# Wide products for ten projection tiles of a block attention, and a longer warming run, in a two-model fp32 kernel

## The chip, the cores and the metric

The kernel runs on one core of one Trainium2 chip as one launch. The metric is the device time of that core in microseconds (us), lower is better; a kernel's time is the median of several executions. One execution was also recorded by the hardware profiler, and all rows below are of that one. Times inside it count from the start of its span.

## The reference

Two transformer-like blocks are applied to one sequence of 256 tokens of width 1024, all in fp32. The first has two gated feed-forward layers around a mixer (Fourier mixing and grouped attention). The second has two layers, and the change is in the attention of its second one:

```python
def shared_kv(x, kv_norm, w_kv, cos, sin):
    k, v = jnp.split(rms_norm_2(x, kv_norm) @ w_kv, 2, axis=-1)
    k = apply_partial_rope(k.reshape(bsz, seq, N_HEADS, HEAD_DIM_2), cos, sin)
    ...
def moba_attention(h, w_q, w_o, cos, sin, k_blk, v_blk, k_mean):
    q = apply_partial_rope((h @ w_q).reshape(bsz, seq, N_HEADS, HEAD_DIM_2), cos, sin)
    ...
x = x + moba_attention(h, moba_w_q[j], moba_w_o[j], cos, sin, k_blk, v_blk, k_mean)
x = x + mem_cross_attention(rms_norm_2(x, norm_mem[l]), rms_norm_2(mem, norm_memkv[l]),
                            mem_w_q[l], mem_w_kv[l], mem_w_o[l])
```

There are 8 heads of 128 and blocks of 256 tokens. The sequence is one block, so each query sees its own block alone, under a causal mask. The keys of the memory attention that follows (`m` below) depend on the memory alone and are projected during the block attention.

## The kernel before

**Tiles and their split.** All weights are laid out by the host as 205 tiles of 128 x 16 x 128 fp32 numbers (1 MB each), in the order in which they are used (`STREAM`). Tile `t` lies in slot `t % 3` of three buffers. For each one SyncE loads `raw`; ScalarE writes the rounded high half to `wt[:, 0]` (`split` of ScalarE, line 972, semaphore `weight_hi`); VectorE writes the remainder `raw - high` to `wt[:, 1]` (`split` of VectorE, line 1340, semaphore `weight_lo`). An operand (`xn`, `mn`, `h`) is held in the same way as a high part and a rest. A product in fp32 accuracy is then high x high + high x rest + remainder x high.

**Wide and narrow.** A tile gives two blocks of 128 outputs (`m`) for 256 tokens and has 8 steps of the inner dimension (`k`). *Wide*, the high weights multiply high part and rest of the operand side by side in one product of 512 columns (line 424), and the remainder multiplies the high part in one of 256 columns (line 482) that lands on the columns of the rest: 16 + 16 products per tile. The bank holds two halves, which have to be added when it is emptied. *Narrow*, all three products have 256 columns and land on the same columns (lines 469 and 482): 48 products per tile, and one instruction empties the bank. In both forms `square_tile` waits for `weight_hi` before its first product and for `weight_lo` before its first product with the remainder. For value tiles the operand is the stationary side and the weights move. Their narrow form (`narrow_values`, lines 504 and 509) waits for `weight_hi` first and for `weight_lo` after its 32 products with the high half. Their wide form (the rest of `value_tile`, lines 527 and 530) moves high half and remainder side by side and waits for `weight_lo` before its first product.

**Emptying.** In the block attention (`moba`) the k and m tiles are emptied by VectorE (`scaled`, line 1469: times the norm factor), and the q and v tiles by ScalarE alone (lines 997 and 1002, semaphore `copied_out`). Wide tiles elsewhere: ScalarE copies the rest half to one of three `rest` buffers (`rest`, lines 984 and 988), VectorE adds it (`whole_of`, line 1460; for values line 1580), and the semaphore `drained` counts them.

**Order in the block attention stage.** Each engine has one program order, written out by hand. The tiles are `MOBA`: k0, k1, v0, q0, q1, k2, q2, v1, k3, q3, v2, v3, m0, m1. TensorE does the first five, then the scores of heads 0 and 1, and from there on the other tiles in pieces (`PIECES`) between the steps of the 8 heads: transposing the probabilities (line 835), the scores of two heads later (line 819), the product with the values (line 847). VectorE gives each q and k tile a rotation (`turn`, lines 1601 to 1604), and for each head takes the maxima, normalises the probabilities (line 1674) and makes the rest of the output (`rest`). Between these stand its splits: `after(t)` is the split of tile t + 2. So the split of tile 5 (k2) stands behind the turn of q0, that of tile 7 (v1) behind the turn of k2, and those of tiles 9 to 13 one each behind the maxima of a head. For a head's scores TensorE waits until its q tile is turned, and for its value product until the v tile is drained.

**Start.** While the first loads are under way, TensorE multiplies `ones` by `ones` `WARM` times (line 856). One such fp32 product shows as two records.

Of the kernel before, what the change touches and what calls it, by code (L numbers as in the profile page):

```python
# [10 lines left out]
ACT = mybir.ActivationFunctionType  # L11
AX = mybir.AxisListType

P = 128
S = 256
# [3 lines left out]
NT = S // P  # L19
TILE = 16  # L20
RING = 3
FF = 22
WARM = 10
KEEP = 7
LAST = 2752 % P
UPPER, LOWER = slice(0, LAST), slice(LAST, P)
# [6 lines left out]
MOBA = [("k", 0), ("k", 1), ("v", 0), ("q", 0), ("q", 1), ("k", 2), ("q", 2), ("v", 1), ("k", 3), ("q", 3), ("v", 2), ("v", 3),  # L33
        ("m", 0), ("m", 1)]
# [13 lines left out]
FIRST, COUNT = {}, {}  # L48
# [26 lines left out]
]  # L75


NARROW = ("w_in", "moba")
PAIR, OUT, EMPTIED, REST, RESTS, TAKEN = {}, {}, {}, {}, [], {}
_taken = 0  # L80
_count, _emptied = {"drained": 0, "copied_out": 0}, {}
for _name, _pairs in PAIRS:
    for _j, _p in enumerate(_pairs):
        PAIR[_name, _j] = _p
        EMPTIED[_name, _j] = _emptied.get(_p)
        if _name in ADD:
            _emptied[_p] = ("added", KP * ADD[_name] + _j + 1)
            continue
        _by = "copied_out" if _name == "moba" and MOBA[_j][0] in "qv" else "drained"
        _count[_by] += 1  # L90
        OUT[_name, _j] = _emptied[_p] = (_by, _count[_by])
        if _name.startswith("gu"):
            _taken += 1
            TAKEN[_name, _j] = _taken
            _emptied[_p] = ("taken", _taken)
        if _name not in NARROW:
            REST[_name, _j] = len(RESTS)
            RESTS.append((_name, _j))

# [53 lines left out]
SPREAD_AT = {n: i + 1 for i, n in enumerate(SPREADS)}  # L153
# [21 lines left out]
def program(nc, weights, x_t, mem_t, vectors, consts, fourier, fnet_w, positions, out_t):  # L175
    ctx = ExitStack()
    with ctx:
# [14 lines left out]
        q_t = sb("q_t", [P, KB, S])  # L192
        k_t = sb("k_t", [P, KB, S])
        v_s = sb("v_s", [P, NT, D])
# [17 lines left out]
        col_x = sb("col_x", [P, NT])  # L212
# [32 lines left out]
        def pair_banks(name, j):  # L245
            return bank[:, 2 * PAIR[name, j]:2 * PAIR[name, j] + 2, :]
# [17 lines left out]
        def pair(b):  # L264
            return slice(2 * b, 2 * b + 2)
# [11 lines left out]
        tile_done = sem("tile_done")  # L277
        taken, rest_copied, drained, copied_out = sem("taken"), sem("rest_copied"), sem("drained"), sem("copied_out")
# [6 lines left out]
        factor, spread, spread_taken = sem("factor"), sem("spread"), sem("spread_taken")  # L285
# [135 lines left out]
        def _(pe):  # L421
# [91 lines left out]
            def value_tile(t, out, a, beside={}, ks=(0, KB), narrow=False):  # L513

                w = wt[t % RING][:].rearrange("p a (m k) c -> p a m k c", m=2)
                if narrow:
                    narrow_values(t, out, a, w, beside, ks)
                    return
                o = [out[:, n, :].rearrange("p (a m c) -> p a m c", a=2, m=2) for n in range(NT)]
                tok = [slice(n * P, (n + 1) * P) for n in range(NT)]  # L520
                if ks[0] == 0:
                    pe.wait_ge(weight_lo, t + 1)
                for k in range(*ks):
                    if k in beside:
                        beside[k]()
                    for n in range(NT):
                        pe.matmul(o[n], a[:, k, 0, tok[n]], w[:, :, :, k, :], start=k == 0, stop=False, skip_group_check=True)  # L527
                for k in range(*ks):
                    for n in range(NT):
                        mm = pe.matmul(o[n][:, 1], a[:, k, 1, tok[n]], w[:, 0, :, k, :], start=False, stop=k == KB - 1,  # L530
                                       skip_group_check=True)
                if ks[1] == KB:
                    mm.then_inc(tile_done, 1)
# [208 lines left out]
            def part(kind, j, ks=(0, KB), **more):  # L742
                what = PARTS[kind][j][0]
                t, out = FIRST[kind] + j, banks_for(kind, j, ks[0] == 0)
                if kind == "moba":
                    src = h[:, KB:2 * KB] if what == "q" else mn if what == "m" else xn
                else:
                    src = xn if what == "q" else mn
                if what == "v":
                    value_tile(t, out, src, ks=ks, beside=more.get("beside", {}), narrow=kind in NARROW)  # L750
                else:
                    square_tile(t, out, src, ks=ks, narrow=kind in NARROW, **more)

            def pieces(kind, n, i, ready):
                for j, k0, k1 in PIECES[kind][n][i]:
# [141 lines left out]
            for j in range(5):  # L897
                square_tile(FIRST["w_in"] + j, banks_for("w_in", j), xn, ready=operand("mix") if j == 0 else None, narrow=True,
                            late=None if j else KP * OPERAND["mix"],
                            beside={**norm("mix").get(j, {}), **sums_beside.get(j, {}), **({4: head_factors} if j == 4 else {})})  # L900
# [6 lines left out]
            for g in range(4):  # L907
                f_s, out = probs[g % 2], seq[g % 2]
# [19 lines left out]
            for j in range(COUNT["conv_in"]):  # L928
                square_tile(FIRST["conv_in"] + j, banks_for("conv_in", j), xn, ready=operand("mix0") if j == 0 else None,
                            cuts=() if j else (4, 6), late=None if j else KP * OPERAND["mix0"],  # L930
                            beside={1: {5: both_sums}, 2: {1: lambda: spread_factor("mix0")}, 3: {1: lambda: spread_column(col_1, SPREAD_AT["mix0 first"], 0)}}.get(j, {}))
# [16 lines left out]
            for j in range(AHEAD["moba"]):  # L948
                part("moba", j, **({0: dict(ready=operand("kv"), late=KP * OPERAND["kv"]), 3: dict(ready=operand("mix1"))}.get(j, {})),
                     beside=norm("mix1").get(j, {}))  # L950
# [10 lines left out]
        def _(act):  # L961
# [15 lines left out]
            def rest(name, j, col=None, factors=0):  # L977

                i, src = REST[name, j], pair_banks(name, j)[:, :, S:2 * S]
                act.wait_ge(tile_done, FIRST[name] + j + 1)  # L980
                if i >= 3:
                    out_of(act, *RESTS[i - 3])
                if col is None:
                    act.activation(rest_s[i % 3][:], src, ACT.Copy).then_inc(rest_copied, 1)  # L984
                else:
                    act.wait_ge(factor, factors)
                    for n in range(NT):
                        e = act.activation(rest_s[i % 3][:, n, :], src[:, n, :], ACT.Copy, scale=col[:, n:n + 1])
                    e.then_inc(rest_copied, 1)

            def rest_part(kind, j):
                what, i = PARTS[kind][j]
                if kind == "moba":
                    src = pair_banks(kind, j)
                    if what == "q":
                        act.wait_ge(tile_done, FIRST[kind] + j + 1)
                        act.activation(q_t[:, pair(i), :], src[:, :, 0:S], ACT.Copy).then_inc(copied_out, 1)
                    elif what == "v":
                        act.wait_ge(tile_done, FIRST[kind] + j + 1)
                        act.wait_ge(factor, SPREAD_AT["mix1"])  # L1000
                        for n in range(NT):
                            e = act.activation(v_s[:, n, 2 * P * i:2 * P * (i + 1)], src[:, n, 0:S], ACT.Copy, scale=col_x[:, n:n + 1])
                        e.then_inc(copied_out, 1)
                elif what != "v":
                    rest(kind, j)
                else:
                    rest(kind, j, col_m, SPREAD_AT["mem"])

# [210 lines left out]
            for j in range(3):  # L1219
                after(FIRST["w_in"] + j)  # L1220
                out_of(act, "w_in", j)
                src = gk_t if j == 0 else q_t[:, 2 * j - 2:2 * j, :]
# [46 lines left out]
            for p in range(KP):  # L1269
                for m in range(2):  # L1270
                    k, j = 2 * p + m, 3 * p + m
# [56 lines left out]
        def _(dve):  # L1328
# [135 lines left out]
                    e.then_inc(told, 1)  # L1464

            def scaled(name, j, dst, r):
                if name in NARROW:
                    dve.wait_ge(tile_done, FIRST[name] + j + 1)
                    dve.tensor_tensor(dst, pair_banks(name, j)[:, :, 0:S], both(r), ALU.mult).then_inc(drained, 1)
                    return  # L1470
                whole_of(name, j, dst)
                dve.tensor_tensor(dst, dst, both(r), ALU.mult).then_inc(drained, 1)
# [97 lines left out]

            def part(kind, j):
                what, i = PARTS[kind][j]
                if OUT[kind, j][0] == "copied_out":
                    return
                of_memory = what == "m" if kind == "moba" else what != "q"
                if what == "v":
                    col, src, at = col_m if of_memory else col_x, pair_banks(kind, j), REST[kind, j]
                    dve.wait_ge(rest_copied, at + 1)
                    for n in range(NT):
                        e = dve.scalar_tensor_tensor(v_s[:, n, 2 * P * i:2 * P * (i + 1)], src[:, n, 0:S], col[:, n:n + 1],  # L1580
                                                     rest_s[at % 3][:, n, :], ALU.mult, ALU.add)
                    e.then_inc(drained, 1)
                elif what == "q":

                    whole_of(kind, j, q_t[:, pair(i), :], drained)
                else:
                    scaled(kind, j, k_t[:, pair(i), :], (r_m if of_memory else r_x)[:])
# [272 lines left out]
            for p in range(KP):  # L1860
                for m in range(2):
                    k, j = 2 * p + m, 3 * p + m
# [18 lines left out]
                j = 3 * p + 2  # L1881
# [66 lines left out]
            m, y, t = (root[:, i, 0:NT] for i in range(3))  # L1948
# [131 lines left out]
```

## Time and profile before

| | before |
|---|---|
| median of 3 executions | 1235.22 us (1235.21 to 1235.88) |
| profiled execution, its own time | 1236.79 us |
| its span, first to last instruction | 1235.0 us |
| TensorE busy (products) | 1227.8 us, 99% |
| VectorE busy | 929.0 us, 75% |
| ScalarE busy | 660.0 us, 53% |
| read from memory | 219.52 MB, 179 GB/s over the span |

The span lies 1.8 us under the profiled execution's own time. Busy shares are means over stages with different limits; the page's slices and the timelines show them stage by stage. The end of a product is modelled, so that neighbouring products overlap in the records: what tells their pace is the distance from start to start.

### The profile page before, as it was taken

What the parts mean: (1) busy time and instruction counts of PE and PEld (TensorE: products, weight loads), DVE (VectorE), ACT (ScalarE), POOL (GpSimd) and SP (SyncE); (2) the same over time, 40 slices, a digit from 0 to 9 for tenths busy, and PEclk for the clock granted to TensorE, in tenths of its full rate; (3) what the DMA queues carried; (4) which work ended last, traced back from release to release, by engine and by line L of the source; (5) the groups of instructions that cost most, each with busy time, mean ns of one, the idle gap of its engine ahead of it and who ended that gap; (6) DMA issues with size and microseconds to landing.
All of it is one profiled execution on the core that took longest, in us unless ns stands there. A gap on an engine that the chain in (4) does not pass through costs nothing.

```text
span 1235.0 us, 18032 instructions
## 1 busy us (share of the span) xinstructions
PE 1227.8 (99%) x7398; PEld 1094.5 (89%) x7398; DVE 929.0 (75%) x1294; ACT 660.0 (53%) x875; POOL 32.9 (3%) x23
## 2 busy tenths in 40 slices
PE   9999999999999999999999999999999999999998
PEld 8888889978888888888888888889998888888887
DVE  7787766869777858988668777669968657877744
ACT  6655544556655444446546555454655445555632
POOL 0000000000000000540000000000000000000000
PEclk9999999999999999999999999999999999999999
DMA  8565664245555663556346555644445533555560
GB/s 293 206 229 174 217 223 157 83 137 185 190 176 199 205 228 113 195 185 219 117 143 233 199 178 191 216 170 162 146 145 187 180 136 137 205 203 174 199 209 35
DMA packets 52114, 221.74 MB, mean 180 GB/s; under 512 B 4640, under 2 KB 6976, under 8 KB 31552
## 3 DMA queue, kind: packets, MB, share of 16 engines
q1 hardware_dynamic: 51744, 220.32, 51.7%
q8 instruction: 59, 0.97, 0.3%
q10 hardware_dynamic: 288, 0.27, 0.1%
q14 instruction: 23, 0.19, 0.0%
HBM read 219.52 MB, written 1.05 MB: 179 GB/s over the span
## 4 chain that ended last, share of the span: by engine, by line
PE 94%; DVE 4%; issue 1%; ACT 1%; DMA 0%; DVEq 0%; ACTq 0%
PE bank L424 41%; PE bank L482 17%; PE bank L444 8%; PE bank L428 7%; PE bank L469 5%; PE bank L438 4%; PE bank L527 2%; PE bank L819 2%; PE bank L847 2%; DVE wt L1340 1%; PE bank L504 1%; PE bank L530 1%; PE bank L509 1%; PE bank L835 0%; PE bank L564 0%
## 5 line engine op out<-in xcount | busy, mean ns | idle before, releaser
L1340 DVE TENSOR_TENSOR wt<-raw,wt 128x2048 fp32r<-128x2048 f32 x202 | 464.2, 2300 | 67.9 <-ACT wt L972 67.4
L972 ACT ACTIVATE wt<-raw 128x2048 fp32r<-128x2048 f32 x202 | 385.9, 1911 | 114.8 <-PE bank L428 62.1
L424 PE MATMUL bank<-xn,wt 128*128 128x512 f32 x1280 | 313.6, 394 | 0.7 <-DVE xn L1725 0.7
L424 PEld LDWEIGHTS bank<-xn,wt 128*128 128x128 f32 x1280 | 236.4, 189 | 48.5 <-issue 1.9
L424 PE MATMUL bank<-h,wt 128*128 128x512 f32 x1004 | 243.9, 392 | 0.0
L424 PEld LDWEIGHTS bank<-h,wt 128*128 128x128 f32 x1004 | 183.5, 188 | 34.9 <-issue 0.4
L482 PEld LDWEIGHTS bank<-xn,wt 128*128 128x128 f32 x1360 | 174.0, 191 | 7.4 <-DVE wt L1340 1.4
L482 PE MATMUL bank<-xn,wt 128*128 128x256 f32 x1360 | 177.4, 283 | 0.1
L1460 DVE TENSOR_TENSOR scratch<-bank,rest 128x512 f32<-128x512 f32 x98 | 67.7, 690 | 84.9 <-ACT rest L984 84.8
L1059 ACT ACTIVATE h<-scratch 128x256 fp32r<-128x256 f32 x88 | 36.8, 418 | 157.5 <-DVE scratch L1500 157.5
L444 PE MATMUL bank<-xn,wt 128*128 128x512 f32 x432 | 103.2, 391 | 0.0
L984 ACT ACTIVATE rest<-bank 128x512 f32<-128x512 f32 x114 | 67.6, 593 | 65.7 <-PE bank L482 48.9
L428 PEld LDWEIGHTS bank<-h,wt 128*128 128x128 f32 x700 | 90.2, 191 | 3.6
L444 PEld LDWEIGHTS bank<-xn,wt 128*128 128x128 f32 x432 | 79.3, 188 | 15.3
L428 PE MATMUL bank<-h,wt 128*128 128x256 f32 x700 | 91.6, 283 | 0.0
L1484 DVE TENSOR_TENSOR scratch<-scratch,r_x 128x512 f32<-128x512 f32 x86 | 59.5, 692 | 2.9
L1011 ACT ACTIVATE xn<-x,vec 128x256 fp32r<-128x256 f32 x62 | 28.1, 501 | 53.7 <-DVE x L1355 53.1
L438 PE MATMUL bank<-xn,wt 128*128 128x256 f32 x432 | 56.4, 283 | 0.0
L438 PEld LDWEIGHTS bank<-xn,wt 128*128 128x128 f32 x432 | 53.9, 192 | 0.0
L482 PEld LDWEIGHTS bank<-h,wt 128*128 128x128 f32 x384 | 50.9, 191 | 2.8
L482 PE MATMUL bank<-h,wt 128*128 128x256 f32 x384 | 52.0, 282 | 0.0
L1354 DVE SCALAR_TENSOR_TENSOR x<-bank,x 128x512 f32<-128x512 f32 (+1 forms) x39 | 24.9, 638 | 29.8 <-PE bank L482 17.3
(232 smaller groups left out, 1129.5 us busy)
## 6 DMA issues: line engine op xcount, KB each, us to landing
raw<-weights SPq DMA_DIRECT2D x158, 1024.0 KB, 4.9
raw<-weights SPq DMA_DIRECT2D x86, 512.0 KB, 5.0
raw<-weights SPq DMA_DIRECT2D x12, 256.0 KB, 4.8
k_t<-mem_t SPq DMA_DIRECT2D x2, 1024.0 KB, 7.0
raw<-weights SPq DMA_DIRECT2D x8, 128.0 KB, 4.4
out_t<-work SPq DMA_DIRECT2D x4, 256.0 KB, 2.3
x<-x_t SPq DMA_DIRECT2D x3, 256.0 KB, 5.4
v_s<-fourier SPq DMA_DIRECT2D x2, 256.0 KB, 5.3
```

The costliest lines, as they stand in the source:

```text
L424: return pe.matmul(out, hi, a.rearrange("p a s -> p (a s)"), start=first, stop=False, skip_group_check=True)
L428: return pe.matmul(out[:, S:2 * S], lo, a[:, 0, :], start=False, stop=last, skip_group_check=True)
L438: pe.matmul(out[:, m, S:2 * S], w[:, 1, m * KB + k, :], a[:, k, 0, :], start=k == 0, stop=False, skip_group_check=True)
L444: mm = pe.matmul(out[:, m, :], w[:, 0, m * KB + k, :], a[:, k].rearrange("p a s -> p (a s)"), start=False, stop=k == KB - 1, skip_group_ch ...
L469: pe.matmul(out[:, m, 0:S], w[:, 0, m * KB + k, :], a[:, k, i, :], start=k == i == 0, stop=False, skip_group_check=True)
L482: mm = pe.matmul(home, w[:, 1, m * KB + k, :], a[:, k, 0, :], start=False, stop=k == KB - 1, skip_group_check=True)
L972: act.activation(wt[t % RING][:, 0], raw[t % RING][:], ACT.Copy).then_inc(weight_hi, 1)
L984: act.activation(rest_s[i % 3][:], src, ACT.Copy).then_inc(rest_copied, 1)
L1059: act.activation(h[:, j, 0, :], gate, ACT.Copy).then_inc(h_rounded, 1)
L1340: dve.tensor_tensor(wt[t % RING][:, 1], raw[t % RING][:], wt[t % RING][:, 0].bitcast(F32), ALU.subtract).then_inc(weight_lo, 1)
L1460: e = dve.tensor_tensor(dst, pair_banks(name, j)[:, :, 0:S], rest_s[i % 3][:], ALU.add)
L1484: dve.tensor_tensor(gu_s[j % 3], gu_s[j % 3], both(r_x[:]), ALU.mult).then_inc(drained, 1)
```

## The change

`NARROW`, a list of kinds of tiles, becomes a function of the tile: of the block attention only the k tiles stay narrow. Its q, v and m tiles (ten) are done wide. Their rest half is copied by ScalarE and added by VectorE, as for wide tiles elsewhere, and `copied_out` has no user left. `WARM` goes from 10 to 12.

```diff
-WARM = 10
+WARM = 12
...
-NARROW = ("w_in", "moba")
+def narrow_tile(name, j):
+    return name == "w_in" or name == "moba" and MOBA[j][0] == "k"
...
-        _by = "copied_out" if _name == "moba" and MOBA[_j][0] in "qv" else "drained"
-        _count[_by] += 1
-        OUT[_name, _j] = _emptied[_p] = (_by, _count[_by])
+        _count["drained"] += 1
+        OUT[_name, _j] = _emptied[_p] = ("drained", _count["drained"])
...
-        if _name not in NARROW:
+        if not narrow_tile(_name, _j):
             REST[_name, _j] = len(RESTS)
...
-                    value_tile(t, out, src, ks=ks, beside=more.get("beside", {}), narrow=kind in NARROW)
+                    value_tile(t, out, src, ks=ks, beside=more.get("beside", {}))
                 else:
-                    square_tile(t, out, src, ks=ks, narrow=kind in NARROW, **more)
+                    square_tile(t, out, src, ks=ks, narrow=narrow_tile(kind, j), **more)
...
-                if kind == "moba":
-                    src = pair_banks(kind, j)
-                    if what == "q":
-                        act.wait_ge(tile_done, FIRST[kind] + j + 1)
-                        act.activation(q_t[:, pair(i), :], src[:, :, 0:S], ACT.Copy).then_inc(copied_out, 1)
-                    elif what == "v":
-                        act.wait_ge(tile_done, FIRST[kind] + j + 1)
-                        act.wait_ge(factor, SPREAD_AT["mix1"])
-                        for n in range(NT):
-                            e = act.activation(v_s[:, n, 2 * P * i:2 * P * (i + 1)], src[:, n, 0:S], ACT.Copy, scale=col_x[:, n:n + 1])
-                        e.then_inc(copied_out, 1)
-                elif what != "v":
+                if narrow_tile(kind, j):
+                    return
+                if what != "v":
                     rest(kind, j)
+                elif kind == "moba":
+                    rest(kind, j, col_x, SPREAD_AT["mix1"])
                 else:
                     rest(kind, j, col_m, SPREAD_AT["mem"])
...
             def part(kind, j):
                 what, i = PARTS[kind][j]
-                if OUT[kind, j][0] == "copied_out":
-                    return
```

## Rows read from the trace of the kernel before

**Rows 1.** The page: busy us and share, then VectorE in tenths of 40 slices.
```profile
PE 1227.8 (99%) x7398; PEld 1094.5 (89%) x7398; DVE 929.0 (75%) x1294; ACT 660.0 (53%) x875; POOL 32.9 (3%) x23
...
DVE  7787766869777858988668777669968657877744
```

**Rows 2.** The page: the chain that ended last, by engine.
```profile
PE 94%; DVE 4%; issue 1%; ACT 1%; DMA 0%; DVEq 0%; ACTq 0%
```

**Rows 3.** TensorE's timeline: start us, us, engine line op out<-in xcount.
```profile
848.05 4.00 PE L469 MATMUL bank<-h,wt 128*128 128x256 f32 x32
...
853.81 4.00 PE L469 MATMUL bank<-h,wt 128*128 128x256 f32 x32
...
941.28 3.82 PE L424 MATMUL bank<-h,wt 128*128 128x512 f32 x16
...
952.41 3.82 PE L424 MATMUL bank<-xn,wt 128*128 128x512 f32 x16
```

**Rows 4.** TensorE's timeline: the scores of heads 0 and 1, and tile 7.
```profile
859.57 1.48 PE L819 MATMUL bank<-k_t,q_t 128*128 128x128 f32 x8
...
873.20 4.18 PE L504 MATMUL bank<-wt,xn 128*128 128x256 f32 x32
```

**Rows 5.** Busy us from 845 to 880 (TensorE, weight loads, VectorE, ScalarE); VectorE's timeline.
```profile
845.00:880.00 35.00, 35.00 (x288) 34.79 (x288) 34.18 (x62) 14.38 (x20) 0.00 (x0) 1.00 0.42 147
...
858.16 0.68 DVE L1604 TENSOR_TENSOR q_t<-q_t,work 32x512 f32<-32x512 f32 x1
...
869.68 0.68 DVE L1469 TENSOR_TENSOR k_t<-bank,r_x 128x512 f32<-128x512 f32 x1
...
870.41 0.74 DVE L1601 STREAM_SHUFFLE work<-k_t 32x512 f32<-32x512 f32 x1
...
873.11 2.27 DVE L1340 TENSOR_TENSOR wt<-raw,wt 128x2048 fp32r<-128x2048 f32 x1
```

**Rows 6.** Groups by line: busy us, mean ns of one, idle before and its releasers.
```profile
L1460 DVE TENSOR_TENSOR q_t<-bank,rest 128x512 f32<-128x512 f32 x8 | 5.5, 692 | 7.6 <-ACT rest L984 7.5
...
L1580 DVE SCALAR_TENSOR_TENSOR v_s<-bank,col_m,rest 128x256 f32<-128x256 f32 x16 | 7.0, 479 | 16.5 <-ACT rest L988 16.5
```

**Rows 7.** VectorE's, then TensorE's timeline, later in the stage.
```profile
882.72 0.17 DVE L1670 RECIPROCAL small<-small 128x2 f32<-128x2 f32 x1 [1.16 <-ACT scratch L1149]
...
893.17 2.29 DVE L1340 TENSOR_TENSOR wt<-raw,wt 128x2048 fp32r<-128x2048 f32 x1
...
900.31 2.28 DVE L1340 TENSOR_TENSOR wt<-raw,wt 128x2048 fp32r<-128x2048 f32 x1
...
906.20 0.55 DVE L1674 TENSOR_SCALAR scratch<-scratch,small 128x128 f32<-128x128 f32 x2
...
910.37 2.29 DVE L1340 TENSOR_TENSOR wt<-raw,wt 128x2048 fp32r<-128x2048 f32 x1
...
895.37 3.70 PE L504 MATMUL bank<-wt,xn 128*128 128x256 f32 x28
...
902.95 3.04 PE L504 MATMUL bank<-wt,xn 128*128 128x256 f32 x24
...
907.27 0.82 PE L847 MATMUL bank<-scratch,v_s 128*128 128x256 f32 x4
...
910.34 2.56 PE L469 MATMUL bank<-mn,wt 128*128 128x256 f32 x20
...
912.74 1.43 PE L482 MATMUL bank<-mn,wt 128*128 128x256 f32 x10
```

**Rows 8.** The start: TensorE's timeline, then VectorE's.
```profile
1.02 4.63 PE L856 MATMUL bank<-ones 128*128 128x128 f32 x20 [1.02 <-POOL weigh L404]
...
6.31 3.75 PE L424 MATMUL bank<-xn,wt 128*128 128x512 f32 x8 [0.66 <-DVE xn L1725]
...
11.11 1.99 PE L424 MATMUL bank<-xn,wt 128*128 128x512 f32 x8
...
20.57 0.16 DVE L1448 TENSOR_SCALAR root<-bank 128x2 f32<-128x2 f32 x1 [1.34 <-PE bank L564]
```

More of the change, by code:

```diff
@@ L1466, in scaled @@
             def scaled(name, j, dst, r):
-                if name in NARROW:
+                if narrow_tile(name, j):
                     dve.wait_ge(tile_done, FIRST[name] + j + 1)
```

## The prediction

> **What bounds the kernel now.** I read the page first. TensorE is busy 99% of the span, and the slices show VectorE at 90% or more in two neighbouring slices of 30.9 us each, the 28th and 29th, that is from 834 to 896 us [rows 1]. That is the stage of the change. The chain that ended last is TensorE for 94% of the span [rows 2]. So a microsecond taken from TensorE's stream is a microsecond of the kernel, and so is a microsecond for which TensorE is made to wait; nothing later has idle time in which to give it back. Then I read TensorE's and VectorE's timelines side by side over the block attention stage, asking of each weight tile at which moment TensorE asks for its remainder (`weight_lo`, line 1340) and at which moment VectorE has made it. I number the tiles by their place in `MOBA`: 2 is v0, 3 q0, 4 q1, 5 k2, 6 q2, 7 v1, 8 k3, 9 q3, 10 v2, 11 v3, 12 m0, 13 m1.
>
> **Part 1, TensorE's own work.** A narrow square tile is 48 products of 256 columns; the next tile starts 5.76 us after it (848.05 to 853.81). A wide one is 16 products of 512 and 16 of 256; from 941.28 to 952.41 are one wide square tile and one wide value tile, 11.13 us for both, 5.57 each [rows 3]. The columns are the same, 12,288; 16 products fewer give 0.19 us, 12 ns for each one left out. Ten tiles change (four q, four v, two m): 10 x 0.19 = **1.9 us less**. The four k tiles stay narrow.
>
> The Trainium skill ("TensorE: Matmul & The Clock Gate", section "Wait — 56ns, not 53.3ns?") puts the fixed cost of a product at about 2.5 ns at the fast clock. By it 160 fewer products would be worth 0.4 us and not 1.9, and the whole sum would end 1.5 us higher. The rows above are these very products, so they decide; the page's figure does not hold for them.
>
> **Part 2, what VectorE gains in work.** Before, ScalarE alone empties the q and v tiles. After, ScalarE copies the rest half to `rest` and VectorE adds the other half. The q addition is the row of `q_t` at line 1460, 0.69 us; a value tile is two of line 1580 at 0.48 us [rows 6], some 0.85 us back to back. What follows a q addition is its turn, which waits for it, as line 1601 waits for line 1469: 869.68 to 870.41, 0.73 us from start to start [rows 5]. For an m tile it is one more 0.69 us. ScalarE's copies are as many and as wide as those that they replace (the m tiles' two come in addition, where ScalarE has idle time); I cost them at nothing.
>
> Before split(7), the remainder of tile 7, VectorE does v0, q0 and q1 in its program order: 0.85 + 0.73 + 0.73 = **2.3 us more**. There is no idle time to take it: from 845 to 880 us it is busy for 34.2 of 35 us [rows 5], with none of the rest a wait for another engine, so all that follows is shifted by the full 2.3 us.
>
> **Part 3, when TensorE asks.** This is the step that decides. A narrow value tile waits for `weight_hi`, does its 32 products with the high half and only then waits for `weight_lo`, 3.8 to 4 us into the tile. The wide `value_tile` waits for `weight_lo` before its first product. For tile 7 the rows say: TensorE starts it at 873.20 [rows 4]; split(7) runs from 873.11 to 875.38 [rows 5]. So even with VectorE's work unchanged the wide form would start 2.2 us late. With 2.3 us more, split(7) ends at 877.7, and with 0.06 us to the first product tile 7 starts at 877.75 and not at 873.20: **4.55 us later** than now. That number already holds what happened before: the four wide tiles 2, 3, 4 and 6 won 0.8 us, and two smaller waits lie inside it. The first is the scores of head 0 at 859.57 [rows 4], which need q0 turned. That is 858.84 now [rows 5], and 0.85 + 0.73 later makes 860.4 where TensorE would be there at 859.0. The second is the remainder of tile 6. Whatever they cost is swallowed by tile 7. Behind tile 7 on TensorE are all later products.
>
> **Part 4, the rest of the stage.** From split(7) on VectorE is 2.3 us late; q2's addition makes it 3.0 at split(8). v1's drain (0.85 us) falls partly into idle time at the softmax of head 2, where VectorE now waits 1.16 us for ScalarE [rows 7], but it must await ScalarE's copy of v1, behind those exponentials; split(9) and split(10) come out 3.6 us late. Split(10) ran 893.17 to 895.45, so it ends at 899.1; tile 10 started at 895.37 [rows 7] and would start at 895.37 + 4.55 less two wide tiles (0.4) = 899.5. It is just in time. q3's addition makes split(11) 4.35 us late: 902.59 + 4.35 = 906.95, against tile 11 at 902.95 + 4.55 - 0.6 = 906.9; a wait of 0.1 us. Then the product of head 4's probabilities with v2 (907.27) needs v2 drained: probabilities of head 6 normalised at 906.7 now [rows 7], 911.05 then, ScalarE's copy in between, v2's two instructions to 912.0. TensorE would be there at 911.2: a wait of 0.8 us. Tile 12 then starts at about 915.1 where it started at 910.34, its split ends at 917.4 and its remainder is asked for at 917.35 (now 910.37 + 2.29 = 912.66 and 912.74 [rows 7]): 0.1 to 0.2 us. The two m tiles win 0.4 us. At the end of the stage TensorE is 4.55 - 4 x 0.19 (tiles 7, 9, 10, 11) + 0.1 + 0.8 + 0.15 - 0.4 = **4.5 us later** than now: waits of some 6.4 us against a gain of 1.9. From there on VectorE has idle time in each head again, so I expect no more waits.
>
> **Part 5, the four warming products.** `WARM` 10 to 12 gives 24 records and not 20. The 20 start from 1.02 us on, 0.21 us apart, and the idle time of 0.66 us before the first real product at 6.31 [rows 8] takes the four more: 4 x 0.213 = 0.85 us after 5.44 is 6.3 us. Directly they cost 0 to 0.1 us. What they change is the pause. The first eight wide products take 3.75 us, the eight of the same shape from 11.11 on 1.99 [rows 8], 0.43 and 0.23 us from one to the next: up to some 10.4 us, in the products of 256 columns between them, TensorE ran at half its clock (the 1.2 GHz of its two levels). It had by then run without a pause since 6.31, some 4.1 us. The warming run without a pause lasted 4.4 us and did not raise it. An unbroken run from 1.02 may raise it anywhere from 5.4 us to, at worst, 10.4 as now. Bounds: no gain (or 0.1 lost), or up to 4.1 us of real work done in half the time. The latter is capped: the statistics' VectorE chain starts at 20.57 after 1.34 us of waiting for TensorE [rows 8], and it runs on into the remainders of tiles 3 to 5 of the first feed-forward, so that no more than about 1.35 us can be kept. I take the middle of the two times, 7.9 us: 2.5 us less at half clock, **1.2 us gained**.
>
> The Trainium skill (same page, section "What's actually happening") says that recent activity releases the throttle, and that the hardware looks on a schedule of its own that does not start with the kernel. By that rule the moment of release differs from run to run, and closing the pause helps in most of them, which is the same sign as my 1.2 us.
>
> **The sum.** +4.5 - 1.2 = +3.3 us. On the profiled execution that is a span of 1235.0 + 3.3 = 1238.3; its own time of 1236.79 lies 1.6 us above the median of the timed runs, which I take as a difference of executions. The median is 1235.22 + 3.3 = **1238.5 us**.
>
> **Rivals.**
> - *No gain from warming (chance 0.22).* The clock rises when it does now. Speaks for it: 4.4 us unbroken had not been enough. 1235.2 + 4.5 + 0.05 = 1239.8 us.
> - *The losses compound (0.06).* VectorE's lag also makes the head-by-head handshakes late (maxima, exponentials, normalising), one more wait of 0.8 us at heads 1 to 3. 1235.2 + 4.5 + 2.4 - 1.2 = 1240.9 us.
> - *VectorE's additions cost less than their rows (0.13).* Only the asking for the remainder is earlier: tile 7 late by 2.2, nothing at tiles 10 to 12; 2.2 - 6 x 0.19 = +1.0 us, less 1.2: 1235.0 us. Against it: no idle row lies ahead of split(7).
> - *Faster (0.09).* The remainders are not late: that needs split(7) done before TensorE gets there, which would be at 872.5; so 2.9 us earlier than the row says and 5.2 us earlier than the sum says. Then 1235.2 - 1.9 - 1.2 = 1232.1 us. It turns on that one remainder: from where split(7) is later than TensorE by 3.1 us the change loses. Only a different order on VectorE than its program would bring it.
> - The forecast has 0.50.
>
> **How the numbers follow.** A measurement of this kernel tells about 0.2%, 2.5 us, from no change, so the bounds are 1232.7 and 1237.7. The forecast's own range is 1237.0 to 1239.8 (warming 0 to 1.35, head 4's wait 0 or not, 0.3 us either way on tile 7); about a tenth of its weight lies within 0.2%. Slower: 0.45 + 0.22 + 0.06 and a little of the third rival, 0.75; same 0.16; faster 0.09. The range of 8 in 10 goes from 1236.3 to 1240.6: it leaves out the faster case and most of the third rival.
>
> **What will show it.** The ten tiles as 16 products at 0.228 us and 16 at 0.12. Idle time of TensorE ahead of tile 7's first product, released by VectorE's line 1340, of 3 to 4 us; a smaller one of about 1.4 us ahead of the scores of head 0, released by the turn of q0; one of 0.8 us ahead of head 4's value product, released by `v_s`. Nothing of the kind in other stages. At the start 24 warming products without a pause to the first real one, and their successors passing from 0.43 to 0.23 us apart before 10.4 us. The forecast is wrong if tile 7 starts less than 3 us later than it did, or if VectorE has idle time before split(7).

## The result, and the profile after

The changed kernel takes 1240.23 us (median of 5, 1239.98 to 1241.45) against 1235.22 before (median of 5): ratio 1.0038, 95% interval 1.0027 to 1.0049, so 0.27 to 0.49% slower. The profiled execution has a span of 1238.2 us and an own time of 1239.98.

The first view is the page: busy time and the chain that ended last.

```profile
PE 1225.9 (99%) x7242; PEld 1084.7 (88%) x7242; DVE 936.1 (76%) x1308; ACT 661.2 (53%) x877; POOL 32.9 (3%) x23
...
PE 87%; DVE 9%; issue 1%; DMA 1%; ACT 1%; SPq 0%; DVEq 0%; ACTq 0%
```

Against [rows 1, 2]: TensorE has 156 fewer products (160 fewer in the tiles, 4 more at the start) and 1.9 us less busy time; VectorE has 7 us more. The share that matters is that of the chain: VectorE's went from 4 to 9%. Next, who made TensorE wait (us in total, times, longest):

```profile
PE bank L529 <- DVE wt L1335: 3.2, 1, 3.2
PE bank L858 <- POOL weigh L406: 1.0, 1, 1.0
PE bank L821 <- DVE q_t L1597: 1.0, 1, 1.0
PE bank L426 <- DVE scratch L1455: 0.6, 1, 0.6
PE bank L849 <- DVE v_s L1573: 0.5, 1, 0.5
```

Three of these are new and lie in the block attention: tile 7's wait for its remainder, the scores of head 0 waiting for q0's turn, head 4's value product waiting for v2. In TensorE's timeline they are the rows that end in brackets. The first row is the start of tile 3, the fourth and the last are the larger pieces of tile 11 and tile 12. The wait for line 1455 is also new; it lies near 30 us, at the start of the kernel, and comes up again below.

```profile
847.00 3.82 PE L426 MATMUL bank<-h,wt 128*128 128x512 f32 x16
...
859.29 1.55 PE L821 MATMUL bank<-k_t,q_t 128*128 128x128 f32 x8 [0.99 <-DVE q_t L1597]
...
876.53 3.91 PE L529 MATMUL bank<-wt,xn 128*128 128x512 f32 x16 [3.19 <-DVE wt L1335]
...
905.66 3.00 PE L529 MATMUL bank<-wt,xn 128*128 128x512 f32 x12
...
910.59 0.92 PE L849 MATMUL bank<-scratch,v_s 128*128 128x256 f32 x4 [0.50 <-DVE v_s L1573]
...
913.72 2.44 PE L426 MATMUL bank<-mn,wt 128*128 128x512 f32 x10
```

And VectorE's side of tile 7: k2's last step of the turn, the split, q2's addition.

```profile
873.50 0.68 DVE L1597 TENSOR_TENSOR k_t<-k_t,work 32x512 f32<-32x512 f32 x1
874.11 2.27 DVE L1335 TENSOR_TENSOR wt<-raw,wt 128x2048 fp32r<-128x2048 f32 x1
876.32 0.67 DVE L1455 TENSOR_TENSOR q_t<-bank,rest 128x512 f32<-128x512 f32 x1
```

The split ends at 876.38, TensorE starts 0.15 later: the wait named is the one that released it.

To compare executions whose starts differ, I measure a **stage**: from the first product of tile 3 to the first value product of the memory attention that follows. Before it is 848.05 to 946.85; the table below gives it for every kernel. TensorE's and the other engines' busy time in it, before and after (us of the stretch; TensorE, weight loads, VectorE, ScalarE):

```profile
848.05:946.85 98.80, 98.80 (x747) 95.29 (x746) 82.14 (x145) 51.29 (x92) 0.00 (x0) 1.00 0.46 160
```

```profile
847.00:950.05 103.05, 98.37 (x602) 87.61 (x601) 89.44 (x159) 52.61 (x94) 0.00 (x0) 1.00 0.43 153
```

The stage grew by 4.25 us while TensorE's busy time in it shrank (a busy record overlaps short waits, so it shrank by less than the products saved). VectorE's grew by 7.3. Tile 2, ahead of the stage, gives 0.2 back: 4.1 us in all.

### The profile page after: what moved, and what is told of

The parts are those of the page before. It is cut to its first block, busy times and chain, and to the rows that moved or that the text cites. A ratio compares the mean times of both kernels' runs of the same rounds, so it can differ in the third digit from the quotient of the medians.

```text
span 1238.2 us, 17742 instructions
## 1 busy us (share of the span) xinstructions
PE 1225.9 (99%) x7242; PEld 1084.7 (88%) x7242; DVE 936.1 (76%) x1308; ACT 661.2 (53%) x877; POOL 32.9 (3%) x23
## 4 chain that ended last, share of the span: by engine, by line
PE 87%; DVE 9%; issue 1%; DMA 1%; ACT 1%; SPq 0%; DVEq 0%; ACTq 0%
PE bank L426 41%; PE bank L484 16%; PE bank L446 8%; PE bank L430 7%; PE bank L440 4%; DVE wt L1335 3%; PE bank L529 2%; PE bank L471 2%; PE bank L849 1%; PE bank L532 1%; PE bank L821 1%; DMA raw<-weights 1%; DVE work L1594 0%; DVE work L1596 0%; PE bank L566 0%
## 5 line engine op out<-in xcount | busy, mean ns | idle before, releaser
L426 PE MATMUL bank<-h,wt 128*128 128x512 f32 x1068 | 259.4, 392 | 0.0
L426 PEld LDWEIGHTS bank<-h,wt 128*128 128x128 f32 x1068 | 195.3, 188 | 37.2 <-issue 0.4
L986 ACT ACTIVATE rest<-bank 128x512 f32<-128x512 f32 x120 | 71.2, 593 | 71.5 <-PE bank L484 56.2
L430 PEld LDWEIGHTS bank<-h,wt 128*128 128x128 f32 x700 | 90.2, 191 | 3.6
L484 PEld LDWEIGHTS bank<-h,wt 128*128 128x128 f32 x384 | 51.0, 191 | 3.4 <-DVE wt L1335 0.4
```

The lines of the kernel that those rows point to most:

```text
L426: return pe.matmul(out, hi, a.rearrange("p a s -> p (a s)"), start=first, stop=False, skip_group_check=True)
L430: return pe.matmul(out[:, S:2 * S], lo, a[:, 0, :], start=False, stop=last, skip_group_check=True)
L484: mm = pe.matmul(home, w[:, 1, m * KB + k, :], a[:, k, 0, :], start=False, stop=k == KB - 1, skip_group_check=True)
```

## The experiments

Theory A: the moment of asking costs, since the wide value tile asks for its remainder at once. Theory B: VectorE's chain of work up to head 4's value product sets the end of the stage, wherever TensorE waits in it; the asking matters only at tile 7. (The chain is not all VectorE's: at heads 2 and 6 VectorE waits 1.16 us for ScalarE's exponentials, which themselves wait for VectorE's maxima.) The stage in us, from one profile each, and the times:

| kernel | stage | to head 4 | median us | ratio to before, 95% |
|---|---|---|---|---|
| before | 98.8 | 59.2 | 1235.2 | |
| changed | 103.1 | 63.6 | 1240.23 | 1.0038 (1.0027 to 1.0049) |
| e1, warming alone | 98.8 | 59.2 | 1235.18 | 0.9995 (0.9987 to 1.0004) |
| e2, wide alone | 104.1 | 64.6 | 1239.88 | 1.0033 (1.0021 to 1.0046) |
| e3, values narrow | 100.8 | 61.3 | 1237.82 | 1.0017 (1.0008 to 1.0026) |
| e4, rest first | 103.0 | 63.6 | 1239.08 | 1.0029 (1.0018 to 1.0039) |
| e5, queries narrow | 102.6 | 63.3 | 1238.95 | 1.0030 (1.0019 to 1.0042) |
| e6, late tiles only | 98.5 | 59.1 | 1235.76 | 1.0002 (0.9993 to 1.0011) |
| e7, small additions | 102.1 | 62.7 | 1238.21 | 1.0021 (1.0012 to 1.0029) |
| e8, filled pause | 103.1 | 63.6 | 1239.96 | 1.0035 (1.0022 to 1.0047) |
| e9, e7 with e4 | 99.1 | 59.6 | 1235.30 | 1.0001 (0.9992 to 1.0010) |
| e10, e6 with warming | 98.5 | 59.1 | 1235.24 | 0.9999 (0.9990 to 1.0008) |

"To head 4" is from tile 3's first product to head 4's value product. The later kernels ran against 21 to 24 executions of the kernel before, with medians of 1235.1 to 1235.4. One of the 11 executions of e3 took 2895.33 us, and nothing on record shows why; the ratio leaves it out, the median counts it (1237.67 without it).

**e1, warming alone.**

```diff
-WARM = 10
+WARM = 12
```

> Only WARM goes from 10 to 12; all tiles as before. Theory 1 (closing the pause lets the clock rise earlier in the usual execution, as the two profiles show): 0.9 us faster than the kernel before. Theory 2 (the profiled execution of before was an unusual one; most of its executions had the early rise already, since its own time lay 1.6 us above the median): no gain in the median, 0 to 0.9 us slower, and the records show the 24 products ahead of a first real product that is at full pace at once.

No gain to be seen in the times, though their interval (1.6 us faster to 0.5 us slower) would also hold theory 1's 0.9 us. The profiles decide for theory 2. In e1 the first eight wide products take 2.42 us where they took 3.75 [rows 8]:

```profile
1.02 5.49 PE L856 MATMUL bank<-ones 128*128 128x128 f32 x24 [1.02 <-POOL weigh L404]
6.16 2.42 PE L424 MATMUL bank<-xn,wt 128*128 128x512 f32 x8
8.42 1.10 PE L428 MATMUL bank<-xn,wt 128*128 128x256 f32 x8
```

But in the seven other profiles with `WARM = 10` (e2 to e7 and e9) these eight took 2.06 to 2.54 us too, behind pauses of 0.3 to 1.2 us. The longest pause is e9's:

```profile
1.02 3.92 PE L879 MATMUL bank<-ones 128*128 128x128 f32 x20 [1.02 <-POOL weigh L410]
6.17 2.08 PE L430 MATMUL bank<-xn,wt 128*128 128x512 f32 x8 [1.23 <-DVE xn L1759]
```

So the early rise is the usual case with 10 warming products as well, and the profile of before is the one of eight without it. (The granted clock of the first 14 us reads 1.00 in all profiles, that of before included; the half pace is read from the products' distance alone.)

Whether the late rise makes the long executions is not shown. Six of the 24 executions of before measured beside e1 lie from 1236.6 to 1236.9, the others from 1235.0 to 1236.0, and the profiled one (1236.79) is like the six; of e1's 11 none lies above 1236.2. But 0 of 11 against 6 of 24 can be chance, and e10's profile took 1236.53 us with the early rise.

**e2, wide alone**: the changed kernel with `WARM = 10`.

> The ten tiles wide, WARM stays 10. Both theories of the warming products: 4.1 us slower by the profiles (TensorE's waits of 3.2, 1.0, 0.5, 0.2 and some smaller ones less 1.9) plus nothing. If theory 1 of warming holds this is 0.9 us slower than the changed kernel; if theory 2 holds it is as slow or up to 0.9 us faster than that. The waits of TensorE on line-1340 splits and on the q0 turn are the same as in the changed kernel.

The median is 4.5 us above that of before, the ratio 1.0033; with the interval it can't be told from the changed kernel. The waits are the same. But its stage is 1.0 us longer than that of the changed kernel, and that is in one place, tile 7's 16 products of 512 columns: 5.35 us from the first to the next pass (876.60 to 881.95) and not 3.75.

```profile
876.60 5.50 PE L533 MATMUL bank<-wt,xn 128*128 128x512 f32 x16 [3.22 <-DVE wt L1348]
881.95 2.08 PE L536 MATMUL bank<-wt,xn 128*128 128x256 f32 x16
```

By stretches (columns as above; the last but two is the granted clock):

```profile
872.00:876.00 4.00, 1.38 (x11) 0.98 (x9) 3.93 (x5) 1.63 (x3) 0.00 (x0) 1.00 0.55 225
876.00:878.00 2.00, 1.40 (x5) 1.19 (x6) 1.92 (x5) 1.37 (x3) 0.00 (x0) 0.87 0.32 57
878.00:880.00 2.00, 2.00 (x6) 1.51 (x6) 1.97 (x4) 0.00 (x0) 0.00 (x0) 0.50 0.92 365
880.00:882.00 2.00, 2.00 (x9) 1.59 (x8) 2.00 (x2) 0.00 (x0) 0.00 (x0) 0.78 0.25 102
```

After the pause of 3.2 us the clock fell to half, 1.2 GHz, and came back within tile 7: 1.6 us lost, of which 0.5 fell where head 4 would have waited for v2 anyway. In the profile of the changed kernel it stayed up after the same pause (1.00 in all four stretches).

**e3, values narrow.** Queries and memory tiles wide, the values as before. `WIDE` names the wide tiles, and narrow q and v tiles are emptied by ScalarE alone:

```diff
-WARM = 12
+WARM = 10
...
+WIDE = [p for p in MOBA if p[0] in "qm"]
...
-    return name == "w_in" or name == "moba" and MOBA[j][0] == "k"
+    return name == "w_in" or name == "moba" and MOBA[j] not in WIDE
```

> Queries and memory tiles wide, values narrow and emptied by ScalarE as before, WARM 10. VectorE has 1.3 us more before the split of tile 7 (ends 876.7), and tile 7 asks for it 4.0 us after its start at about 873. If the loss comes from the early asking of the wide value tiles together with VectorE's added work: no wait at tile 7, one of at most 0.5 us at tile 6's remainder, total 0.3 to 0.8 us faster than before. If VectorE's added work for the queries (turn late for the scores) is the main cause: 1 to 2 us slower.

There is no wait at tile 7, yet the kernel is 2.1 us slower by the ratio (the stage 1.96 longer): the expectation's first theory missed, its second (1 to 2 us slower) holds. Who waits is new:

```profile
PE bank L853 <- DVE h L1689: 1.1, 2, 0.9
...
PE bank L853 <- ACT v_s L1008: 0.6, 1, 0.6
```

Line 853 is the value product. For head 3's it waits for VectorE's rest of head 2's output; for head 4's it waits for ScalarE's copy of v2, which stands behind exponentials that wait for VectorE's maxima. Both fit theory B, by which the sum is simple: the four additions of 0.65 us on average that VectorE does before the maxima of head 6 are 2.6 us, the kernel before had 0.57 us to spare there (v2 copied at 906.7, the product at 907.27), and 2.6 - 0.57 = 2.0; measured 61.28 - 59.21 = 2.07.

**e4, rest first.** The wide kernel of e2; `value_tile` gets a branch for the block attention that takes the products in another order:

```diff
+                rest_first = FIRST["moba"] <= t < FIRST["moba"] + COUNT["moba"]
+                if rest_first:
+                    if ks[0] == 0:
+                        pe.wait_ge(weight_hi, t + 1)
+                    for k in range(*ks):
...
+                        for n in range(NT):
+                            pe.matmul(o[n][:, 1], a[:, k, 1, tok[n]], w[:, 0, :, k, :], start=k == 0, stop=False, skip_group_check=True)
+                    if ks[0] == 0:
+                        pe.wait_ge(weight_lo, t + 1)
+                    for k in range(*ks):
+                        for n in range(NT):
+                            mm = pe.matmul(o[n], a[:, k, 0, tok[n]], w[:, :, :, k, :], start=False, stop=k == KB - 1, skip_group_check=True)
...
+                    return
```

> As the wide-only kernel, but the four value tiles do their 16 products of high weights with the operand's rest first (they need weight_hi alone) and ask for weight_lo 1.9 us later. Theory A (the moment of asking is what costs): the wait at tile 7 falls from 3.2 to 1.2 us and 2 us come back, so about 2.1 us slower than before. Theory B (VectorE's chain of work runs unbroken from 844 us to the draining of v2 at 910 us and sets the end of the stage, wherever TensorE waits): the wait only moves, to the products of head 4 with v2 and the remainders of tiles 10 and 11, and the time is within 0.5 us of the wide-only kernel, 3.6 to 4.1 us slower than before.

As theory B says: tile 7's wait falls by 2 us, and head 4's product starts at the same moment.

```profile
876.47 3.93 PE L540 MATMUL bank<-wt,xn 128*128 128x512 f32 x16 [1.20 <-DVE wt L1365]
...
902.23 0.89 PE L870 MATMUL bank<-scratch,v_s 128*128 128x256 f32 x4 [0.73 <-DVE h L1706]
...
910.61 0.92 PE L870 MATMUL bank<-scratch,v_s 128*128 128x256 f32 x4 [1.63 <-DVE v_s L1605]
```

910.61 here, 910.59 in the changed kernel. The 2 us are paid at heads 3 and 4. What holds head 4 is the end of VectorE's chain, v2's addition; in the changed kernel it is this row, and here it starts at 909.68:

```profile
909.66 0.88 DVE L1573 SCALAR_TENSOR_TENSOR v_s<-bank,col_x,rest 128x256 f32<-128x256 f32 x2
```

The times leave a question open. e4's median is 0.8 us below e2's and 1.15 us below the changed kernel's, although the stage of the profile is that of the changed kernel. The intervals of the ratios overlap; fewer falls of the clock after a shorter pause would give the same sign, but no run separates that.

**e5, queries narrow**: as e3, with `p[0] in "vm"`.

> Values and memory tiles wide, queries narrow and emptied by ScalarE as before, WARM 10. Theory B (VectorE's chain up to head 4, with what TensorE waits for at tile 7): before the split of tile 7 VectorE has 0.8 us more (v0), so it ends at 876.2 and tile 7 starts 3.0 us later than before; v1 and v2 add 1.7 us more up to head 4, less than that wait. From the first product of tile 3 (q0) to head 4's value product 61.6 to 61.8 us (59.22 before, 63.59 in the changed kernel), at the end 2.1 us slower than before. If the queries' additions are the whole cost: as fast as before or faster.

Slower by 3.7 us (ratio 1.0030) where 2.1 was expected. Tile 7's wait is 2.5 us, no other new one; the first product of tile 7 stands 28.3 us after tile 3's, 3.2 more than before, as expected within 0.2. Up to head 4 it is 1.5 us more than expected, and the clock, which fell here too, accounts for it: 5.2 us for the 16 products and not 3.75.

```profile
875.76 5.37 PE L533 MATMUL bank<-wt,xn 128*128 128x512 f32 x16 [2.48 <-DVE wt L1348]
880.97 2.07 PE L536 MATMUL bank<-wt,xn 128*128 128x256 f32 x16
```

**e6, late tiles only**: `WIDE = (v3, m0, m1)`, with e4's order of products and `WARM = 10`.

> Only v3, m0 and m1 wide (v3 with the operand's rest first), all else as before, WARM 10. Theory B: VectorE's added work comes after head 4's value product, where it has idle time; so no wait is added but 0.1 us at m0's remainder. From tile 3's first product to head 4's value product 59.2 us as before less 0.1, and 0.4 to 0.5 us less than before by the second output tile. Time 0.4 us under the kernel before, which the times can hardly tell from none. If wide tiles cost in themselves: 1 us slower or more.

The stage is 0.34 us shorter than before, as expected within 0.1, with no wait added; in the times it can't be seen. So wide tiles are cheaper in themselves (e10's profile shows the same 98.5 us), and the loss is in what they ask of VectorE ahead of head 4's value product.

**e7, small additions.** All ten wide; VectorE adds two columns of a query or value tile of the block attention, the rest of each addition is left out:

```diff
+                    if kind == "moba":
+                        dve.scalar_tensor_tensor(v_s[:, 0, 2 * P * i:2 * P * i + 2], src[:, 0, 0:2], col[:, 0:1],
+                                                 rest_s[at % 3][:, 0, 0:2], ALU.mult, ALU.add).then_inc(drained, 1)
+                        return
...
+                elif what == "q" and kind == "moba":
+                    at = REST[kind, j]
+                    dve.wait_ge(rest_copied, at + 1)
+                    dve.tensor_tensor(q_t[:, 2 * i, 0:2], pair_banks(kind, j)[:, 0, 0:2], rest_s[at % 3][:, 0, 0:2],
+                                      ALU.add).then_inc(drained, 1)
```

> The ten tiles wide, WARM 10, but VectorE's additions for the block attention's queries and values touch two columns of one half only, so the outputs of that attention are not the reference's; every wait stays. It isolates the asking for the remainder ahead of the first product from VectorE's added work. VectorE is at most 0.6 us later at tile 7's split, which ends at about 876: tile 7 starts 2.6 to 2.8 us later than before, no wait at the scores of head 0 beyond 0.3 us, none at head 4's value product; 61.3 us from tile 3 to head 4, 1.6 to 1.8 us slower than before. If the early asking were harmless without the added work: 1.5 us faster than before.

Tile 7 started 27.85 us after tile 3 (25.15 before): 2.7 later, as expected, with 0.3 us of added work left on VectorE up to split(7) (29.45 us from `r_x`'s copy, 29.16 before). So the asking makes tile 7 wait with hardly any added work.

```profile
874.08 5.51 PE L533 MATMUL bank<-wt,xn 128*128 128x512 f32 x16 [2.88 <-DVE q_t L1598]
```

The row names q2's short addition, which ended at 874.00; the tile waits for its split, which ended at 873.93. The stage is 3.3 us longer and not 1.7 because the clock fell in this execution as well (5.34 us for the 16 products). The eleven executions point the same way: the four with a mean clock of 1.000 took 1236.3 to 1238.2 us, the four with 0.998 1237.5 to 1238.7, the three with 0.997 or less 1238.8 to 1240.2.

**e8, filled pause.** The changed kernel with products of ones ahead of tile 7's wait:

```diff
+                if t == FIRST["moba"] + 7:
+                    for i in range(12):
+                        pe.matmul(out[:, 0, 0:P], ones[:], ones[:], start=True, stop=True)
                 if ks[0] == 0:
                     pe.wait_ge(weight_lo, t + 1)
```

> The changed kernel (all ten wide, WARM 12) with 12 more products of ones by ones into tile 7's own bank ahead of its wait, 2.6 us in TensorE's pause of 3.2. If the pause alone lets the clock fall now and then, as in the profiled wide-only run (16 products of tile 7 in 5.35 us and not 3.75): no fall, the times' spread narrower (1240 us and above gone) and the median 0 to 0.7 us below the changed kernel's 1240.2. If the pause is harmless: the same times, or up to 0.3 us slower by the products. The stage's waits stay.

The pause that is left is 0.42 us and the clock did not fall in the profile, but 1239.96 (1239.33 to 1240.29) against 1240.23 (1239.98 to 1241.45) is no clear difference in 5 executions each, and two of the five still lie above 1240. Inconclusive for the time.

**e9, both**: e7's additions and e4's order.

> Both causes taken away: the ten tiles wide, WARM 10, VectorE's additions for the block attention's queries and values on two columns of one half only (outputs of that attention are not the reference's), and the value tiles do the products with the operand's rest first. Theory B: a wait of 1.2 us at tile 7, no fall of the clock, nothing at head 4; from tile 3's first product to the first of the memory attention's tiles 98.2 to 98.5 us (98.79 before, 103.05 in the changed kernel, 102.09 with small additions alone, 103.04 with the rest first alone). So each mending alone gives little and both together 4.6 us. If the two were independent, the sum of their single effects would give 102.1 less nothing: about 102 us. Time 0.3 us below the kernel before.

The stage is 99.1 us: 0.6 more than expected, but far from 102. The wait at tile 7 was expected, the one of 0.4 us at head 4 for v2 was not:

```profile
874.50 3.94 PE L540 MATMUL bank<-wt,xn 128*128 128x512 f32 x16 [0.89 <-DVE wt L1365]
...
906.42 0.92 PE L870 MATMUL bank<-scratch,v_s 128*128 128x256 f32 x4 [0.38 <-DVE v_s L1605]
```

Small additions alone (e7) leave 3.3 us of loss, 1.6 of them the clock; the later asking alone (e4) leaves 4.2; both together leave 0.3.

**e10, late tiles and warming**: e6 with `WARM = 12`.

> Only v3, m0 and m1 wide as in the late-only kernel, with WARM 12: the version that both sets of runs point to. The stage 98.45 us as in the late-only kernel, 0.34 less than before; no execution with the late clock of the start, so none above 1236.5. Median 1234.8 to 1235.3 against 1235.1 to 1235.4 of before: at most 0.03% faster, within what can be told from none. If the extra warming products cost: 0.5 us slower.

As expected in the stage; 1235.24 against 1235.34, no measurable difference. The version to which the experiments point saves 0.34 us in 1235, less than a measurement tells. One of 11 executions reached 1236.53, so the part on the highest times was not quite right.

## Why the prediction was right or wrong

It forecast +3.3 us (1238.5) with 1236.3 to 1240.6; measured +5.0 by medians, +4.7 by the ratio. The time lies inside the wide range, but outside the forecast's own (1237.0 to 1239.8), and is nearest to the first rival (no gain from warming, 1239.8). The direction, the wait that decides at tile 7 and its size were right; the gain from warming was not there in the median. The span of the two profiles did what the sum said, 1235.0 to 1238.2 where 1238.3 was forecast. That is in part luck: the profile before was the one with the late rise, and the loss (4.1 for 4.5) and the gain (0.9 for 1.2) were both smaller than said.

- **TensorE's own work, 1.9 us less.** Right: tiles 3 and 4 take 5.57 us each (847.00 to 852.57), and the clean case, three late tiles, gave 0.34 of the 0.57 us. The 2.5 ns that the Trainium skill ("TensorE: Matmul & The Clock Gate", section "Wait — 56ns, not 53.3ns?") gives as the fixed cost of a product does not fit these rows either, which come out at 12 ns for each product left out.
- **VectorE 2.3 us later at tile 7.** A little too much. From `r_x`'s copy to split(7) it took 31.1 us after (842.99 to 874.11) and 29.2 before, so 2.0 more: v0's addition cost 0.8, q0's 0.5 and q1's 0.7 net.
- **Tile 7.** Forecast 4.55 us later, measured 4.24 (against tile 1's first product, 835.83 and 836.74). The wait and its releaser are as named, 3.2 us; so are the scores of head 0, 1.0 us where 1.4 was said. e7 shows that the early asking with hardly any added work is already worth 2.7 us, counted from tile 3 (4.4 in the changed kernel).
- **The rest of the stage.** Forecast 4.5 us in all, measured 4.1. Head 4's wait for v2 was 0.5 and not 0.8, tile 12's 0.1. What the prediction did not see is that these small waits are the visible end of a second bound. It took tile 7 for the cause of the loss; e4 removed 2 us there and the stage stayed as long, because VectorE's chain reaches head 4 at the same moment in any case. The two bounds do not add up: VectorE's added work with the later asking costs the whole 4.2 us (e4), the early asking with hardly any added work 1.7, or 3.3 where the clock falls (e7).
- **Warming, 1.2 us gained.** This step failed. The first products do reach full pace earlier and the two profiles differ by 0.9 us at the first tiles of the stage, but the profiled execution of before was an unusual one: in seven of the eight profiles with 10 warming products the pace is early too, behind a pause of up to 1.2 us. Nor did 24 products close the pause in the changed kernel: 0.38 us remained. The own time of the profile of before, 1.6 us above the median, was in the prediction and was put down to "a difference of executions"; the late rise may be a part of that difference, so pricing it against the median counted on something that most of the profiles do not have. e1: no gain to be seen in the median.
- **What is left.** 4.1 us in the stage against 4.7 to 5.0 in the times. The interval of the ratio is 3.3 to 6.1 us, so the difference may be none. Falls of the clock after tile 7's pause (1.0 us of stage in e2's profile) and start-up waits differ from execution to execution. The changed kernel's profile has 0.6 us of waiting for VectorE's line 1455 near 30 us, e10's 0.6, e6's 0.9, e1's none. How much each makes of a remainder was not settled.

## What to carry to other kernels

Before work is moved from one engine to another, add up the receiving engine's program up to each point where someone waits for it; its slack at the last such point (here 0.57 us of 59) is all that is free, and mending the wait that shows moves the loss to the next. When a cheaper form of an operation asks for an input earlier, price that apart from its own time. When the one profiled execution lies off the median, find out in what before pricing an edit at that place.

## What the runs showed of the hardware that was not expected

A pause of TensorE can be followed by a slower clock. After pauses of 2.5, 2.9 and 3.2 us (e5, e7, e2) the granted clock went to half and 16 products took 5.2 to 5.35 us and not 3.75, while after 3.2 us in the changed kernel, 1.2 us in e4 and 0.9 us in e9 it stayed. So a pause of the same length cost 1.6 us more in one execution than in another. That the pause is what lets the clock fall is likely, since no profile without it shows a fall there, but e8, made to show it, was inconclusive. The Trainium skill ("TensorE: Matmul & The Clock Gate", section "What's actually happening") has two clock levels and a hardware schedule that does not start with the kernel. These rows show the two levels (a granted clock of 1.00 and of 0.50) and fit the second, in that equal pauses end differently, but do not show the schedule itself.

At the start, early full pace can meet the next bound: in e10 TensorE then waited 0.9 us for ScalarE's rounding of the first weights, at 9.9 us (0.4 us in e3, nothing in e1 and the changed kernel).

```profile
5.96 2.09 PE L430 MATMUL bank<-xn,wt 128*128 128x512 f32 x8 [0.28 <-DVE xn L1750]
7.89 1.11 PE L434 MATMUL bank<-xn,wt 128*128 128x256 f32 x8
9.90 2.08 PE L430 MATMUL bank<-xn,wt 128*128 128x512 f32 x8 [0.90 <-ACT wt L1216]
```
